# A state-space scan whose decay exponents are built by picking products, and first q, k, v products that are 512 columns wide

## The reference

```python
h = rms_norm(x, norm1_g[l])
z, xbc, dt_raw, q, k, v, g_ssd, g_attn = split(h @ w_in[l])
xbc = silu(causal_dwconv(xbc, conv_w, conv_b))          # xs, Bm, Cm
dt = softplus(dt_raw + dt_bias); A = -exp(a_log)
# chunks of 128 tokens, 32 heads of 64, 8 groups of 4 heads, state 128
a_cs = cumsum(dt * A, axis=-1)
Ldec = exp(where(causal, a_cs[..., :, None] - a_cs[..., None, :], -inf))
CB = einsum('bclgn,bcsgn->bcgls', Cc, Bc)
y_diag = einsum('bcgkls,bcsgkp->bclgkp', CB[:, :, :, None] * Ldec, xs * dt)
states = einsum('bclgn,bcgkl,bclgkp->bcgkpn', Bc, exp(a_cs[..., -1:] - a_cs), X)
y_off = einsum('bclgn,bcgkpn,bcgkl->bclgkp', Cc, prev, exp(a_cs))
y = y_diag + y_off + d_skip * xs
```

## Time and profile before

| | |
|---|---|
| median of the runs shown (lowest, highest) | 2067.77 us (2066.23, 2068.99) |
| profiled execution, its span (the page gives no other time of it) | 2064.5 us |
| PE busy | 1977.9 us, 96% |
| DVE busy | 1661.1 us, 80% |
| ACT busy | 1303.0 us, 63% |
| mean granted TensorE clock | 0.985 |
| DMA | 498.78 MB, mean 242 GB/s |

### The profile page before, as it was taken

One profiled execution on the slowest core, in us unless ns is written; L12 is line 12 of the kernel. 1 busy time (PEld: TensorE's weight loads), 2 busy tenths in 40 slices (PEclk: granted clock), 3 DMA queues, 4 the chain that ended last, 5 costly groups with the idle time before them and its releaser, 6 DMA issues. The chain is left out here.

```text
span 2064.5 us, 28277 instructions
## 1 busy us (share of the span) xinstructions
PE 1977.9 (96%) x11261; PEld 1713.4 (83%) x11261; DVE 1661.1 (80%) x2113; ACT 1303.0 (63%) x1943; POOL 0.2 (0%) x4
## 2 busy tenths in 40 slices
PE   9879999988999999999999999989999999999999
PEld 8668788877778888888888888869988789989997
DVE  6876898677689989998999899978755667767884
ACT  3644534366678777787878787856565745536662
POOL 0000000000000000000000000000000000000000
PEclk9988999999999999999999999999999999999999
DMA  8625799741269989998999899955422444334553
GB/s 334 224 103 184 279 371 327 267 148 41 102 247 369 361 328 353 367 368 331 358 357 363 333 363 360 355 188 184 164 103 102 163 163 144 123 106 147 189 184 111
DMA packets 70810, 498.78 MB, mean 242 GB/s; under 512 B 8080, under 2 KB 8336, under 8 KB 11408
## 3 DMA queue, kind: packets, MB, share of 16 engines
q1 hardware_dynamic: 69952, 494.28, 64.7%
q10 hardware_dynamic: 720, 2.62, 0.3%
HBM read 495.82 MB, written 1.05 MB: 241 GB/s over the span
## 5 line engine op out<-in xcount | busy, mean ns | idle before, releaser
L352 DVE TENSOR_TENSOR wlo<-ring,whi 128x1024 fp32r<-128x1024 f32 (+1 forms) x845 | 1014.9, 1216 | 230.5 <-ACT whi L400 210.5
L400 ACT ACTIVATE whi<-ring 128x1024 fp32r<-128x1024 f32 (+1 forms) x845 | 884.1, 1054 | 469.5 <-PE ps L244 385.9
L244 PE MATMUL ps<-whi,hT 128*128 128x256 f32 (+2 forms) x944 | 315.1, 334 | 9.1 <-DVE wlo L352 3.9
L244 PE MATMUL ps<-whi,hTl 128*128 128x256 f32 (+2 forms) x944 | 309.4, 328 | 0.0
L244 PE MATMUL ps<-wlo,hT 128*128 128x256 f32 (+2 forms) x944 | 309.4, 328 | 0.0
L244 PE MATMUL ps<-whi,xg 128*128 128x512 f32 (+1 forms) x768 | 289.4, 377 | 1.3 <-DVE wlo L352 1.1
L244 PE MATMUL ps<-whi,xgl 128*128 128x512 f32 (+1 forms) x768 | 285.8, 372 | 0.0
L244 PE MATMUL ps<-wlo,xg 128*128 128x512 f32 (+1 forms) x768 | 285.5, 372 | 0.0
L244 PE MATMUL ps<-whi,hf 128*128 128x512 f32 x528 | 208.3, 395 | 4.8 <-DVE wlo L352 3.0
L244 PEld LDWEIGHTS ps<-whi,hT 128*128 128x128 f32 x944 | 180.4, 191 | 31.8 <-DVE wlo L352 7.7
L244 PE MATMUL ps<-wlo,hf 128*128 128x512 f32 x528 | 205.7, 390 | 0.0
(11 more groups left out here) (298 smaller groups left out, 2625.0 us busy)
## 6 DMA issues: line engine op xcount, KB each, us to landing
ring<-in_wstream SPq DMA_DIRECT2D x454, 1024.0 KB, 5.3
work<-in_wstream SPq DMA_DIRECT2D x8, 1024.0 KB, 14.5
ring<-in_wstream SPq DMA_DIRECT2D x4, 832.0 KB, 14.5
modrow<-in_gates ACTq DMA_DIRECT2D x3, 512.0 KB, 6.9
ring<-in_wstream SPq DMA_DIRECT2D x6, 256.0 KB, 2.6
cst<-in_cst SPq DMA_DIRECT2D x1, 1028.0 KB, 26.0
x<-in_x SPq DMA_DIRECT2D x1, 1024.0 KB, 10.3
work<-in_bias ACTq DMA_DIRECT2D x2, 512.0 KB, 4.8
```

Of the source, the lines that this page charges most:

```text
L244: i = self.e.matmul(out, lhsT, rhs, start=start, stop=stop, skip_group_check=True)
L352: i = self.e.tensor_tensor(K.wlo[:, q % NS, 0:cols], src, hi.bitcast(F32), ALU.subtract)
L400: i = self.e.activation(K.whi[:, q % NS, 0:cols], K.ring[:, m % RING, at:at + cols], ACT.Copy)
```

## The change

The decay exponent of head h, a_cs[t] - a_cs[s], is built in another way. `a_` is copied twice side by side (`twice`, 64 columns), and at block 23 two more products with `U` turn the cumulated steps: 64 rows (32 heads, twice) by 256 tokens. ACT writes them as fp32r into `acs_rows`, and DVE replaces the lower 32 rows by the rest that the rounding left. `pick_head` holds two stacked identities of 32; one column of it, broadcast to 128 columns and used as the stationary operand, picks head h's high and low row in one product and lays it on all 128 partitions, on top of the mask. The other sum, which belongs to the partition, is the exponential's bias (`acs_neg`). So `steps` and `aU` are gone, and the exponential is one instruction per head and chunk.

The loop runs over eight groups instead of 16 units: both chunks of a group together, four heads in two pairs (hp), banks 0 to 3 for the exponents, 4 and 5 for B by C, 6 (i = 0) and 7 (i = 1) for the outputs of every group. The first q, k, v go 512 columns wide: the two token halves have a bank each (`QKV0`), and the six units are evicted in pairs.

```diff
@@ plan()
-        p += narrow("qkv0", w, (0,), c, c + 512)
+        p += panels("qkv0", w, (0,), KT, c, c + 512)
@@ new: pe_halves; act_halves evicts both halves when u is odd
+def pe_halves(K, pe, key, u0, u1, banks):
+    for u in range(u0, u1):
+        pair = banks[u // 2]
+        if u % 2 == 0:
+            for b in pair:
+                pe.take(b)
+        k = 4 * (u % 2)
+        for q in K.parts[key][2 * u:2 * u + 2]:
+            q, hi, lo, blocks = pe.chunk()
+            for j in range(len(blocks)):
+                o = slice(512 * j, 512 * j + 512)
+                for i, b in enumerate(pair):
+                    pe.mm3(K.ps[b][:, :], hrows(K)(k, i), (hi[:, o], lo[:, o]), k == 0, k == KT - 1,
...
-QKV0 = (5, 4)
+QKV0 = ((0, 1), (2, 3), (6, 7))
@@ pe_ssd, at_block 23
                 pe.mm(K.ps[4][:, 32 * i:32 * i + 32], K.cst("U"), a_[:, i, :], True, True)
+                pe.mm(K.ps[4][0:64, 128 + 128 * i:256 + 128 * i], K.twice[:, i, :], K.cst("U"), True, True)
@@ pe_ssd: units 0 | transposes | 1, 2 | states | 3 | scores(0), products(0), products(1) | 4, 5 | scores(1) | loop
+    def scores(g):
+        for hp in range(2):
+            b = 2 * (g % 2) + hp
+            pe.take(b)
+            pe.mm(K.ps[b][:, :], K.masks[:, 0, :], K.masks[:, 1, :].unsqueeze(1).to_broadcast([128, 4, 128]), True, False)
+            for hh in range(2):
+                h = 4 * g + 2 * hp + hh
+                pe.mm(K.ps[b][:, 256 * hh:256 * hh + 256], K.pick_head[:, h:h + 1].to_broadcast([64, 128]), K.acs_rows, False, True,
+                      done=("seg", g, hp) if hh else None)
+            pe.given(b, (K.act, ("expE", g, hp)))
...
+    for g in range(8):
+        for i in range(2):
+            pe.take(6 + i)
+        for hp in range(2):
+            pe.wait_ge(K.dve, ("W", g, hp))
+            for h in (2 * hp, 2 * hp + 1):
+                for i in range(2):
+                    pe.mm(K.ps[6 + i][:, 64 * h:64 * h + 64], ET[g % 2][:, h, i, :],
+                          (K.XS if i else K.XD)[:, 256 * g + 64 * h:256 * g + 64 * h + 64], True, True,
+                          done=("diag", g) if h == 3 and i == 0 else None)
+        pe.mm(K.ps[7][:, 256:512], xbc[:, 24 + g, 128:256], st[:, g, :], True, True, done=("off", g))
+        for i in range(2):
+            pe.given(6 + i, (K.dve, ("y", g, i)))
+        if g < 6:
+            scores(g + 2)
+            products(g + 2)
@@ act_ssd
+        if j == 24:
+            a.wait_ge(K.pe, "acs")
+            a.act(K.acs_rows, K.ps[4][0:64, 128:384], ACT.Copy, key="acs rows", own=False)
+    def decay(g):
+        if g >= 2:
+            a.wait_ge(K.pe, ("off", g - 2))
+        for hp in range(2):
+            a.wait_ge(K.pe, ("seg", g, hp))
+            for hh in range(2):
+                h = 2 * hp + hh
+                for i in range(2):
+                    o = 256 * hh + 128 * i
+                    a.act(ET[g % 2][:, h, i, :], K.ps[2 * (g % 2) + hp][:, o:o + 128], ACT.Exp,
+                          bias=K.acs_neg[:, i, 4 * g + h:4 * g + h + 1], key=("expE", g, hp) if hh and i else None, own=False)
@@ dve_ssd: weigh(g, hp) multiplies 2 heads of both chunks (512 columns); out(g) does both chunks
+    for g in range(8):
+        if g < 7:
+            weigh(g + 1, 0)
+            weigh(g + 1, 1)
+        out(g)
```

More of the change, by code:

```diff
@@ L2285, in act_project, with act_halves @@
         a.act(dst[:, :, n0:n0 + 256], K.ps[banks[u % len(banks)]][:, :].rearrange("p (i n) -> p i n", i=2), fn, key=(key, "rows", u), own=False)
+def pe_halves(K, pe, key, u0, u1, banks):
[11 more added lines that the diff above has]
+                    pe.mm3(K.ps[b][:, :], hrows(K)(k, i), (hi[:, o], lo[:, o]), k == 0, k == KT - 1,
+                           done=("w", q) if i and j == len(blocks) - 1 else None)
+                k += 1
+        if u % 2:
+            for i, b in enumerate(pair):
+                pe.given(b, (K.act, (key, "rows", u // 2, i)))
+def act_halves(K, a, key, u0, u1, banks, dsts):
+    for u in range(u0, u1):
+        q = K.parts[key][2 * u + 1]
+        a.split_to(min(q + 1 + NS, K.fence(q)))
+        if u % 2:
+            a.wait_ge(K.pe, ("w", q))
+            for i, b in enumerate(banks[u // 2]):
+                a.act(dsts[u // 2][:, i, :], K.ps[b][:, :], ACT.Copy, key=(key, "rows", u // 2, i), own=False)
 def dve_project(K, v, key, u0, u1):
@@ L2346, in pe_ssd @@
         pe.given(b, (K.act, ("st", g)))
-    pe_project(K, pe, "qkv0", 3, 5, QKV0)
+    pe_halves(K, pe, "qkv0", 3, 4, QKV0)
     pe.wait_ge(K.act, "masks")
[L2350 to L2362, removed]
+    pe.wait_ge(K.dve, "acs")
@@ L2363, in pe_ssd, with products @@
+    def products(g):
+        b = 4 + g % 2
+        pe.take(b)
+        for i in range(2):
+            tc = slice(128 * i, 128 * i + 128)
+            pe.mm(K.ps[b][:, tc], xbc[:, 16 + g, tc], xbc[:, 24 + g, tc], True, True, done=("cb", g) if i else None)
+        pe.given(b, (K.dve, ("W", g, 1)))
     scores(0)
+    products(0)
+    products(1)
+    pe_halves(K, pe, "qkv0", 4, 6, QKV0)
     scores(1)
[L2365 to L2382, removed]
+    pe.wait_ge(K.act, ("st", 7))
@@ new lines, in pe_ssd @@
+    pe.wait_ge(K.dve, "XD1")
+    for g in range(8):
[14 more added lines that the diff above has]
+            products(g + 2)
@@ L2415, in act_ssd @@
         a.act(Brow[:, 128 * q0:128 * q0 + 512], K.ps[K.bank.get(("B", q0), 4)][:, :], ACT.Copy, key=("B", q0), own=False)
[L2417 to L2431, removed]
+    def decay(g):
[5 more added lines that the diff above has]
+                h = 2 * hp + hh
+                for i in range(2):
+                    o = 256 * hh + 128 * i
+                    a.act(ET[g % 2][:, h, i, :], K.ps[2 * (g % 2) + hp][:, o:o + 128], ACT.Exp,
+                          bias=K.acs_neg[:, i, 4 * g + h:4 * g + h + 1], key=("expE", g, hp) if hh and i else None, own=False)
+    act_halves(K, a, "qkv0", 1, 3, QKV0, K.rows0)
     for g in range(8):
@@ L2434, in act_ssd @@
         a.act(st[:, g, :], K.ps[6 + g % 2][:, 0:256], ACT.Copy, key=("st", g), own=False)
-    steps(0)
-    steps(1)
-    act_project(K, a, "qkv0", 3, 5, QKV0, K.rows0)
+    act_halves(K, a, "qkv0", 3, 4, QKV0, K.rows0)
     decay(0)
[L2439 to L2446, removed]
+    act_halves(K, a, "qkv0", 4, 6, QKV0, K.rows0)
+    for g in range(1, 8):
+        decay(g)
 def dve_ssd(K, v):
@@ L2463, in dve_ssd @@
             v.tt(dt, dt, tmp, ALU.add)
-            v.stt(a_, dt, -1.0, K.arow[:, :].unsqueeze(1).to_broadcast([128, 2, 32]), ALU.mult, ALU.mult, key="a")
+            v.stt(a_, dt, -1.0, K.arow[:, :].unsqueeze(1).to_broadcast([128, 2, 32]), ALU.mult, ALU.mult)
+            for n in range(2):
+                v.copy(K.twice[:, :, 32 * n:32 * n + 32], a_, key="a" if n else None)
         if j == 24:
-            v.wait_ge(K.pe, "acs")
+            v.wait_ge(K.act, "acs rows")
             v.copy(acs, K.ps[4][:, 0:64].rearrange("p (i h) -> p i h", i=2))
-            v.tt(tmp[:, 0, :], K.ps[4][:, 64:96], acs[:, 0, :], ALU.subtract, key="acs")
+            v.ts(K.acs_neg, acs, -1.0, None, ALU.mult)
+            v.tt(tmp[:, 0, :], K.ps[4][:, 64:96], acs[:, 0, :], ALU.subtract)
+            v.tt(K.acs_rows[32:64, :], K.ps[4][32:64, 128:384], K.acs_rows[32:64, :].bitcast(F32), ALU.subtract, key="acs")
     dve_project(K, v, "qkv0", 0, 1)
@@ L2484, in dve_ssd, with weigh, out @@
     v.tt(heads(X[:, 1, :]), heads(X[:, 1, :]), wide(K.row("dsk")), ALU.mult)
[L2486 to L2503, removed]
-    dve_project(K, v, "qkv0", 5, 6)
[L2505 to L2508, removed]
+    def weigh(g, hp):
+        E = ET[g % 2][:, 2 * hp:2 * hp + 2, :, :]
+        v.wait_ge(K.act, ("expE", g, hp))
+        v.wait_ge(K.pe, ("cb", g))
+        v.tt(E, E, K.ps[4 + g % 2][:, 0:256].rearrange("p (i t) -> p i t", i=2).unsqueeze(1).to_broadcast([128, 2, 2, 128]), ALU.mult,
+             key=("W", g, hp), own=False)
+    def out(g):
+        y = [X[:, i, 256 * g:256 * g + 256].rearrange("p (h d) -> p h d", h=4) for i in range(2)]
+        t3 = K.rtmp[:, 0:256].rearrange("p (h d) -> p h d", h=4)
+        v.wait_ge(K.pe, ("diag", g))
+        v.tt(y[0], K.ps[6][:, 0:256].rearrange("p (h d) -> p h d", h=4), y[0], ALU.add, key=("y", g, 0), own=g == 0)
+        v.wait_ge(K.pe, ("off", g))
+        v.tt(t3, K.ps[7][:, 256:512].rearrange("p (h d) -> p h d", h=4),
+             eac[:, 1, 4 * g:4 * g + 4].unsqueeze(2).to_broadcast([128, 4, 64]), ALU.mult)
+        v.tt(y[1], K.ps[7][:, 0:256].rearrange("p (h d) -> p h d", h=4), y[1], ALU.add, key=("y", g, 1))
+        v.tt(y[1], y[1], t3, ALU.add)
+    weigh(0, 0)
+    weigh(0, 1)
+    dve_project(K, v, "qkv0", 5, 6)
+    for g in range(8):
[3 more added lines that the diff above has]
+        out(g)
 def turned_y(K):
```

13 lines of the change are left out of this document (8 added, 5 removed).

## The result

The changed kernel is slower by 0.6%, a small difference but clear of the noise: median 2079.80 us of 20 runs (2067.76 to 2098.75) against 2068.57 of 20 (2063.18 to 2078.64) of the kernel before, ratio 1.0058, 95% interval 1.0036 to 1.0079. The forecast was 2058.6, range 2054.5 to 2064.5. The spread doubled, and it goes with TensorE's mean granted clock, which each run reports: 10 of the 20 runs have a clock of 0.972 or less and take 2084 to 2099 us (median 2090.4), the other 10 have 0.977 to 0.980 and take 2068 to 2075 (median 2070.5). So even the runs with the higher clock are not faster than the kernel before. One run of after_again (4976.55 us) and two of the kernel before in its batch (2463 and 2803 us) were disturbed and are in no median, ratio or clock given here.

What follows compares the result with a forecast made beforehand. PE, busy 96% of the span, was taken as the bound. Loop -6.8, ahead of it -0.78, wide q, k, v -1.6, turned sums +0.44 and states -0.46 gave -9.2 us: 2058.6 us forecast, range 2054.5 to 2064.5.

Steps and rivals of the forecast that it cites:

- the picking product's weight: Scan loop: one column read 128 times, 64 rows deep; 0.12 us per product taken, at worst 0.22, costing 3.2 us.
- My chain of waits: Scan loop: PE waits for ACT and DVE at banks 6 and 7, put at 4.0 us in all.
- The clock, rival of 0.05: Scan loop: new waits at banks 6 and 7 bring the mean clock to 0.6, time 2076.8 us; chance 0.05.
- loop at 2.4 GHz: Loop over the scan's groups: 27.3 us of PE work plus 4.0 of waits, 31.3 against 38.11, -6.8 us.
- a group on PE: Scan loop: PE's work for one group of two units falls from 4.84 us to 3.66.
- exponential: Scan loop on ACT: 128 columns with a bias column, 0.29 us each, within 0.25 to 0.45.
- wait, group 0 / 1 / 7: Scan loop: PE waits 1.2, 0.8 and 1.6 us before these groups' products, for ACT's evictions and DVE's work.
- ahead of the loop: Before the loop: one turning and two groups of B by C, 1.91 us instead of 2.69, -0.78 us.
- wide q, k, v, ten chunks: Products for q, k, v, 512 columns instead of 256: 0.16 us less for each of ten chunks, -1.6 us.
- turned sums at block 23: Block 23: two turned cumulations of the steps added on PE, fp32, 64 rows, 128 columns, +0.44 us.
- states: States' stage: one ACT eviction falls behind the states' copy, as units are emptied in pairs, -0.46 us.
- transposes' stage: Transposes: PE's 2.27 us wait for ACT goes, but DVE's copy of the second bank ends the stage as before: 0.

Runs made afterwards that it cites:

- after_again: The changed kernel run again without any edit; 2078.51 us against 2070.09 for the kernel before, ratio 1.0036.
- rows128: The changed kernel with picking products over 128 rows instead of 64, the lower 64 rows picking with zeros; 2063.60 us, ratio 0.9970.
- before_wait: The kernel before with four extra ACT copies that PE waits for before the first unit's products; 2074.35 us, ratio 1.0021.
- fill_wait: The changed kernel with two dense fp32 products, results unused, in front of group 0's products; 2066.42 us, ratio 0.9980.
- before_fill: The kernel before with five dense fp32 products, results unused, behind the first bank of transposes; 2070.99 us against 2069.28, ratio 1.0009.
- mid_dense: The changed kernel with ten dense fp32 products, results unused, in front of group 3's products; 2075.70 us, ratio 1.0044.
- after: The changed kernel itself, against the kernel before; median 2079.80 us against 2068.57, ratio 1.0058.
- wait64: The changed kernel (64-row pickings) with three extra ACT copies that PE waits for before group 0's products; 2090.85 us, ratio 1.0123.
- wait64_dense: The changed kernel with three extra ACT copies that PE waits for before group 0, and ten dense products ahead of group 3; 2088.06 us, ratio 1.0114.

## Why the prediction was wrong

The sum -9.2 us failed at two steps.

1. **"The other unknown is the picking product's weight ... I take 0.12, since type and size are those of rows 5."** Not the type, nor the broadcast column, but the 64 rows were what differed. The two picking products of a bank are 0.22 apart, the next product starts 0.20 to 0.21 after the second, and the first starts 0.32 to 0.43 after its mask product: 1.61 us a turning against 1.03. The bound of 3.2 us that I gave was too small as well, since the change between 128 and 64 rows costs beside the product itself; seven turnings in the loop and one ahead of it make 4.6 us. With 128 rows a turning is 0.93 (1515.43 to 1516.36 in rows128). The term of the loop that failed is thus the turning. My chain of waits was also off, though in the kernel's favour: the wait that I had before group 1 does not show.
2. **The clock, rival of 0.05.** I argued against it by PE's busy share, "87% of the new loop, more than the 72% of the transposes' stage". In the loop at 1.2 GHz PE is busy 100% of 27 us, and the clock stays low all the same. Busy in this record says that an instruction is under way, and here it is no measure of what brings the clock back. The row that I had, 0.95 us of waiting in the old loop at a clock of 1.00, was a row of another loop: before_wait shows that the old one stands 2.97 us. The rival's mechanism was the right one in that a wait at banks 6 and 7 starts it; what I did not see is that the products decide the rest, 58 us instead of a short fall. It costs the profiled execution 24 us (loop 58.5 against 34.4 in fill_wait). The rival's time, 2076.8, lies near the measured median by luck: it supposed a mean clock of 0.6 in every run, while the median stands between runs around 2070.5 and runs around 2090.4.

Apart from the fall, step 1 is nearly all of the miss: in fill_wait masks to z is 177.3, which is 4.7 us less than before (3.8 less than in before_fill) where 9.2 were forecast; the turnings cost 4.6 more than I had, the turned sums 0.5, and shorter waits give a little back. Open is why the runs of the changed kernel with the higher clock do not show even these 4.7 us in their median: none of them has a profile.

The other terms, from the same profiles, were these:

| step | forecast | measured |
|---|---|---|
| loop at 2.4 GHz | 31.3 us (its waits, as printed, add up to 3.9, not 4.0) | 34.4 (fill_wait), 32.1 (rows128) |
| a group on PE | 3.66 | 4.38; 3.60 with 128 rows |
| exponential | 0.29 | 0.25 |
| wait, group 0 / 1 / 7 | 1.2 / 0.8 / 1.6 | 0.8 / none / 1.1 (the last two in fill_wait); with 128 rows 1.4 / 0.4 / 1.3 |
| ahead of the loop | -0.78 | 2.52 - 2.54 = -0.02 (before: 1518.28 to 1520.82, the products' own starts) |
| wide q, k, v, ten chunks | -1.6 | -1.5 (10.99, 5.69 and 11.00 against 11.62 and 17.53) |
| turned sums at block 23 | +0.44 | +0.96 (1.67 from the start of the last product ahead to that of the first behind, before 0.71) |
| states | -0.46 | -0.49 (4.70 against 5.19) |
| transposes' stage | 0 | +0.14 (10.19 against 10.05) |

That the transposes' stage came out at about 0 is only in part by the forecast's reasoning. The wait for the evicted rows is gone, but PE waits 2.12 us for ACT's copy of the first transposed bank, which stands behind a table load (1.28) and two splits (1.99), and only then, 0.91, for DVE's copy that I had named.

"Ahead of the loop" failed by the turning too: 1.61 + 0.91 for B by C, where I had 1.03 + 0.88, and 0.15 because I took the stretch before too long.

The turned sums were off by a shape for which I had no row, like the picking: their weight has 64 columns and alternates with 128-column ones, four changes for 0.5 us. In rows128, where it has 128, they add 0.45 (1.16 between the products around them), which is the forecast. What rests on rows of the same shape held, and with 128 rows, before its short fall at the end, the loop was within 1 us of the forecast.

Left open: why a wait of 1.40 us with 128 rows and one of 2.97 in the old scan did not bring the clock down while 0.81 with 64 rows did in about half of the runs. The same wait of 0.81 us was followed by a fall 1.9 us after its end in the first profile, 0.9 us after in after_again's, and by none in mid_dense's. The products around it may be the reason, but that is not shown, nor which products of the loop keep the clock low: of them only the pickings were varied.

## What to carry to other kernels

Before a short product replaces a dense one, look for a row with the same number of rows and columns in the array, not only the same type and width; if there is none, pad it to 128 with zeros, which here cost nothing (a picking product went from 0.21 to 0.12 us). A busy PE in the record is no sign that its clock is safe: this loop, with many thin products (64 rows, or 64 columns), was 100% busy at 1.2 GHz and stayed there until dense ones came. Where such a loop starts behind a wait, try filling the wait with dense products; here no run fell to 0.972 with it (0 of 12), and 5 of 11 did without.

## What the runs showed of the hardware that I had not expected

- An fp32r product of 256 columns over 64 rows takes 0.20 to 0.22 us from start to start (after), over 128 rows 0.12 (rows128), both at a granted clock of 1.00 and with the same broadcast weight.
- The granted clock stayed at 1.2 GHz for 58.0 us in three profiles of the 64-row loop (after, after_again, wait64), each time until 2 to 4 us into z's products (128 rows, 512 columns), 27.3 us where dense ones came earlier, and 6.8 us in the same place with 128 rows.
- A loop that does not bring the clock back can hold it at 1.00: 34 us in fill_wait, 36 us in mid_dense with its wait of 0.81 us (and ten dense products within), and groups 3 to 6 in wait64_dense.
- An exponential of 128 columns from PSUM with a bias column takes 0.25 us from start to start. The Trainium skill ("ScalarE: Activation LUTs", "What ACT_TABLE_LOAD costs") gives 0.29 as the estimate in the prediction works it out from its formula; the trace does not agree, and the measured number decides.
